# Prompt attention: gated heads first, stick and top-k heads in turn behind them, one output bank for each kind

## The chip, the cores and the metric

One core of a Trainium2 chip. The metric is the device time of one launch in microseconds, the median of the runs. TensorE multiplies and transposes, VectorE and ScalarE read its results from PSUM, GpSimd works on SBUF alone, and SP (SyncE) issues most of the DMA transfers. Each engine takes its instructions in the order in which the program lists them, and waits on semaphores.

## The reference

One step of a decoder layer for a prompt of 512 tokens and for 8 samples of 8 tokens over 4096 cached positions. Three groups of heads work on one projection of the normalised input: 4 stick-breaking heads, 6 heads with an index that selects 128 keys per query of the prompt, and 6 heads that add a compressed, a selected-block and a window branch with sigmoid gates. For the prompt it is, cut to what matters here:

```python
# stick-breaking, no softmax
z = q @ k.T * scale                                   # causal: k_pos < q_pos
log_keep = where(causal, log_sigmoid(-z), 0)
log_after = cumsum(log_keep, reverse=True) - log_keep
o_sb = where(causal, exp(log_sigmoid(z) + log_after), 0) @ v
# top-k ("dsa")
score = sum_heads(relu(iq @ ik.T) * iw)               # causal; top k keys of each query
o_dsa = softmax(q @ k_sel.T * scale + bias) @ v_sel
# gated ("nsa")
o_nsa = g0 * o_cmp + g1 * o_slc + g2 * o_win          # each a softmax with bias
out = concat(o_sb * silu(g_sb), o_dsa * silu(g_dsa), o_nsa * silu(g_nsa)) @ w_out
y = x + rmsnorm(out)
```

## The kernel before

The program does the projection, then the samples' attention, then `prompt_prepare`, `prompt_attention` and `finish` (the output projection with the norm). Each of these is a block of its own: all engines come together between two of them.

**`prompt_prepare`** turns 26 query and key tiles and 16 gate tiles of the projection, two at a time from 21 transfers (`PROMPT_LOADS`, a ring of 4 buffers), all issued by SP. ScalarE makes the sigmoids of the gates (Exp, Ln, Exp), VectorE multiplies them into `kept.oT` (L2291), and both copy the turned tiles. The index scores (`score`) are made between the tiles. The position bias of the twelve softmax heads comes in two transfers of six heads each (L2163): heads 6 to 11, the gated ones, ahead of load 10, and heads 0 to 5, the top-k ones, ahead of load 15. `mask` (L2277) adds the causal mask to the part of the bias that lies on the diagonal, on VectorE.

**`prompt_attention`** works through a list of 112 units. A unit is one head, one tile of 128 queries (`tile` 0 to 3, so 128 to 512 keys wide) and one branch:

- 16 stick units (4 heads);
- 72 gated units: for each of 6 heads and 4 tiles `slc`, `win`, `cmp`;
- 24 top-k units, `dsa` (6 heads), which need the finished top-k search.

Every engine runs one loop over the list. In iteration u:

- TensorE: score of u (L2438 to L2448) into one of 3 banks, turn of u-3 (L2463, L2460), product of u-5 with the values (L2477, L2474) into an `ov` bank;
- VectorE: `add(u)`, `invert(u-1)`, its copies of turned tiles of u-3 (L2497), the product with the gate when a head ends (L2634, six units behind), then its share of the top-k search (`best`, L2616 MAX8 and L2620 MATCH_REPLACE8: 96 steps in all, spread over the first 84 units);
- ScalarE: `exp(u)`, `exp_stick(u-2)`, its copies of u-3;
- GpSimd: `normalise(u-1)` for softmax units, and the padding of the window units.

A softmax unit goes: score, `add` on VectorE (logits plus bias with the maximum, L2589, signals `maxed`), one exp with its sum on ScalarE (L2542, waits for `maxed`), reciprocal on VectorE (L2606), normalisation on GpSimd (L2510, signals `ready`), turn. A stick unit goes: score, Abs, Exp, Ln on ScalarE (L2535 to L2537), three steps on VectorE (L2575 to L2579, signals `soft_dve`), one exp on ScalarE (L2546), turn. In code:

```python
def add(x):                                  # VectorE, a stick
    dve.wait_ge(soft_act, 3 * x.u + 3)       # ScalarE's Ln
...
def exp(x):                                  # ScalarE, a softmax unit
    act.wait_ge(maxed, x.u - n_stick + 1)
```

The output banks `ov[0]` and `ov[1]` alternate from head to head. The SP queue of this block copies the new rows of the caches to the outputs and loads the first three pieces of the output weights.

Of the kernel before, what the change touches and what calls it, by code (L numbers as in the profile page):

```python
# [20 lines left out]
ALU = mybir.AluOpType  # L21
ACT = mybir.ActivationFunctionType
AX = mybir.AxisListType

P = 128
D = 2048
SEQ = 512
# [2053 lines left out]
def prompt_prepare(nc, io, kept, keep):  # L2081
# [15 lines left out]
    with ExitStack() as ctx:  # L2097
# [14 lines left out]
        rows_in = kept.prompt_in  # L2112
        small_in, mask_in, bias_in = s.sem("small_in"), s.sem("mask_in"), [s.sem(f"bias_in{i}") for i in range(2)]
        biased, pad_step = s.sem("biased"), s.sem("pad_step")
# [140 lines left out]
        def _(dve):  # L2255
# [16 lines left out]

            def mask(first, at):

                dve.wait_ge(bias_in[0 if first else 1], 16)
                b = kept.bias[:, first:first + 6, at:at + P]
                dve.tensor_tensor(b, b, pm[:, at:at + P].unsqueeze(1).to_broadcast([P, 6, P]), ALU.add).then_inc(biased, 1)  # L2277

            def gate(i, n):
                if n == 13:  # L2280
                    mask(6, 0)
                    mask(6, SEQ)
                if n == 15:
                    mask(0, SEQ)
                if n == 16:
# [64 lines left out]
def prompt_attention(nc, io, kept, keep):  # L2350


    units = []
    for h in range(4):
        for i in range(4):
            units.append(Unit("stick", h, i, h, h, h, None, None, True, True))
    n_stick = len(units)
    for h in range(6):
# [19 lines left out]
    with ExitStack() as ctx:  # L2378
# [9 lines left out]
        cleared, scored, padded, maxed, exped, rcp_ready, ready = (  # L2388
            s.sem(n) for n in ("cleared", "scored", "padded", "maxed", "exped", "rcp_ready", "ready"))
        turned, copied, multiplied, out_done = s.sem("turned"), [s.sem("copied_dve"), s.sem("copied_act")], s.sem("multiplied"), s.sem("out_done")  # L2390
        soft_act, soft_dve, small = s.sem("soft_act"), s.sem("soft_dve"), s.sem("small")
# [5 lines left out]

        by_act = [u % 2 if u < n_stick else int(u % 3 > 0) for u in range(N)]

# [27 lines left out]
        def _(pe):  # L2427
            def score(x):
                if x.u >= SB:

                    before = units[x.u - SB]
                    if before.kind == "stick":
                        pe.wait_ge(soft_dve, 3 * before.u + 3)
                    else:
                        pe.wait_ge(maxed, before.u - n_stick + 1)
                q = kept.qT[:, x.q, x.tile * P:(x.tile + 1) * P]
# [14 lines left out]
            def turn(x):  # L2451
                if x.kind == "stick":
                    pe.wait_ge(exped, x.u + 1)
                else:
                    pe.wait_ge(ready, x.u - n_stick + 1)
                if x.u >= TB:
# [43 lines left out]
        def _(pool):  # L2500
# [3 lines left out]
            def normalise(x):  # L2504
                if x.kind == "stick":
                    return
                pool.wait_ge(rcp_ready, x.u - n_stick + 1)
                v = view(x)
# [3 lines left out]
            for u in range(N + 1):  # L2512
                if u < N and units[u].kind == "win":

                    pool.wait_ge(turned, u - LB + 1)
                    x = units[u]
# [6 lines left out]
        def _(act):  # L2523
# [3 lines left out]
            def exp(x):  # L2527
                if x.kind == "stick":

                    act.wait_ge(scored, x.u + 1)  # L2530
                    if x.u >= 2:

                        act.wait_ge(soft_dve, 3 * x.u - 3)
                    t = softs[x.u % 2][:, 0:x.w]
# [4 lines left out]
                act.wait_ge(maxed, x.u - n_stick + 1)  # L2539
                if x.kind == "win" and x.off:  # L2540
# [3 lines left out]
            def exp_stick(x):  # L2544
                act.wait_ge(soft_dve, 3 * x.u + 3)
                act.activation(view(x), view(x), ACT.Exp).then_inc(exped, 1)  # L2546

            for u in range(N + TURN):

                if u < n_stick:  # L2550
                    exp(units[u])
                if 2 <= u <= n_stick:
                    exp_stick(units[u - 2])
                if u == n_stick:
                    exp_stick(units[u - 1])
                if n_stick <= u < N:
                    exp(units[u])
                if u >= TURN and by_act[u - TURN]:
                    copy(act, units[u - TURN])

        @block.vector
        def _(dve):
            chain = Links(small)
            def add(x):
# [6 lines left out]
                if x.kind == "stick":  # L2571
                    t = softs[x.u % 2][:, 0:x.w]
                    z = sc[x.u % SB][:, 0:x.w]
                    dve.wait_ge(soft_act, 3 * x.u + 3)
                    dve.scalar_tensor_tensor(t, z, 0.0, t, ALU.max, ALU.add).then_inc(soft_dve, 1)  # L2575
                    dve.wait_ge(soft_dve, 3 * x.u + 1)
                    dve.tensor_tensor_scan(t[:, ::-1], t[:, ::-1], t[:, ::-1], 0.0, ALU.add, ALU.bypass).then_inc(soft_dve, 1)
                    dve.wait_ge(soft_dve, 3 * x.u + 2)
# [12 lines left out]
            def invert(x):  # L2591
                if x.kind == "stick":
                    return
                dve.wait_ge(exped, x.u + 1)
                r = rcp[:, x.u:x.u + 1]
# [26 lines left out]
            for u in range(N + MUL + 1):  # L2622
# [6 lines left out]
                if u - MUL - 1 in outs:  # L2629
# [3 lines left out]
                    to = kept.oT[:, x.out, :].rearrange("p (m t) -> p m t", m=4)  # L2633
                    dve.tensor_tensor(to, to, ov[place[x.out] % 2][:], ALU.mult).then_inc(out_done, 1)  # L2634
                if u < n_free:
                    for n in range(ops_until(u - 1), ops_until(u)):
                        best(n)
                if n_free - 4 <= u < n_free - 1:
                    i = u - (n_free - 4) + 1
# [389 lines left out]
```

## Time and profile before

| what | us |
|---|---|
| median of 3 runs (lowest, highest) | 2465.31 (2464.78, 2466.41) |
| the profiled execution, its own time | 2466.94 |
| its span, first to last instruction | 2465.1 |
| TensorE busy in it (mean granted clock 0.956) | 2276.2 |
| VectorE, ScalarE, GpSimd busy | 941.9, 856.5, 503.0 |
| attention of the prompt, from 2056.5 | 177.0 |

All times of rows are microseconds from the start of the span of one profiled execution. "PEclk" is the share of TensorE's full clock that was granted. In a group, "busy, mean ns of one | idle before it <- who ended that" follow each other; L numbers are lines of the kernel.

### The profile page before, as it was taken

How to read it: one execution, taken by the hardware profiler on the slowest of the kernel's cores; microseconds unless marked ns; L12 is line 12 of the kernel's file. 1: busy time of each engine (PE TensorE's matmuls, PEld its weight loads, DVE VectorE, ACT ScalarE, POOL GpSimd, SP SyncE). 2: the span in 40 equal slices, each digit the busy share in tenths (PEclk: the TensorE clock that was granted, in tenths of full speed). 3: DMA queues.
4: the chain of work that ended last, by engine and by line, in shares of the span. 5: the costliest groups of instructions: out<-in, count | busy, mean ns of one | idle time of the engine just before them, and what ended most of it. 6: DMA issues, size and time to landing. Idle time of an engine off the chain costs nothing. (4 is left out here: it accounts for less than half of the span.)

```text
span 2465.1 us, 46128 instructions
## 1 busy us (share of the span) xinstructions
PE 2276.2 (92%) x16622; PEld 1758.9 (71%) x16625; DVE 941.9 (38%) x1657; ACT 856.5 (35%) x1913; POOL 503.0 (20%) x403
## 2 busy tenths in 40 slices
PE   6999999999999999986999999788799867998996
PEld 3887777777777777764899999555555544777885
DVE  5111121212121212133588886533333348876123
ACT  4000332232222232211444443355455466662000
POOL 5433222222222222212200000000000000444332
PEclk7999999999999999998999999899899876999998
DMA  4755676767676767547666664899999876002423
GB/s 148 213 174 200 232 258 211 262 232 259 226 262 212 264 233 256 186 117 217 182 195 196 194 194 138 270 376 380 308 381 380 284 227 201 1 1 95 124 82 119
DMA packets 322723, 523.15 MB, mean 212 GB/s; under 512 B 36981, under 2 KB 128518, under 8 KB 320662
## 3 DMA queue, kind: packets, MB, share of 16 engines
q1 hardware_dynamic: 302722, 491.76, 60.0%
q10 hardware_dynamic: 16416, 23.13, 2.8%
q0 software_dynamic: 3360, 5.33, 0.6%
q8 instruction: 133, 2.18, 0.4%
q14 instruction: 92, 0.75, 0.1%
HBM read 497.83 MB, written 44.00 MB: 220 GB/s over the span
## 5 line engine op out<-in xcount | busy, mean ns | idle before, releaser
L549 POOL TENSOR_TENSOR proj_w_lo<-kept_region,proj_w_hi 128x1024 fp32r<-128x1024 f32 (+1 forms) x120 | 281.9, 2350 | 723.1 <-DVE proj_w_hi L796 723.1
L576 PE MATMUL proj_acc<-proj_w_hi,h_hi 128*128 128x512 f32 (+1 forms) x958 | 392.6, 410 | 0.0
L578 PE MATMUL proj_acc<-proj_w_lo,h_hi 128*128 128x512 f32 (+1 forms) x958 | 371.6, 388 | 0.0
L577 PE MATMUL proj_acc<-proj_w_hi,h_lo 128*128 128x512 f32 (+1 forms) x958 | 371.3, 388 | 0.0
L748 ACT COPY proj_kT<-proj_tp 128x512 f32<-128x512 f32 x256 | 150.4, 587 | 402.0 <-PE proj_tp L637 347.3
L796 DVE CAST proj_w_hi<-kept_region 128x1024 fp32r<-128x1024 f32 (+1 forms) x120 | 86.8, 726 | 385.5 <-PE proj_acc L580 382.8
L576 PEld LDWEIGHTS proj_acc<-proj_w_hi,h_hi 128*128 128x128 f32 x958 | 180.6, 189 | 60.9 <-issue 31.7
L578 PEld LDWEIGHTS proj_acc<-proj_w_lo,h_hi 128*128 128x128 f32 x958 | 180.2, 188 | 37.9
L577 PEld LDWEIGHTS proj_acc<-proj_w_hi,h_lo 128*128 128x128 f32 x958 | 181.1, 189 | 28.1
L1202 ACT COPY cmp_xT<-cmp_tp 128x512 f32<-128x512 f32 x260 | 139.0, 588 | 160.4 <-PE cmp_tp L1115 160.4
L637 PE MATMUL proj_tp<-kept_consts,kept_region 128*128 128x128 f32 x1024 | 153.5, 272 | 0.0
L637 PEld LDWEIGHTS proj_tp<-kept_consts,kept_region 128*128 128x128 f32 x1024 | 126.2, 140 | 35.5 <-ACT proj_kT L748 5.9
L1115 PE MATMUL cmp_tp<-kept_consts,kept_second 128*128 128x128 f32 x1040 | 139.3, 279 | 5.8 <-DMA kept_second<-in_cache_nsa_kv_dram 4.6
L974 DVE MAX8 kept_top<-kept_scores 64x8 f32<-64x4104 f32 x32 | 141.6, 4423 | 0.5
L976 DVE MATCH_REPLACE8 kept_scores<-kept_top,kept_scores 64x4104 f32<-64x4104 f32 x32 | 141.1, 4409 | 0.0
L1115 PEld LDWEIGHTS cmp_tp<-kept_consts,kept_second 128*128 128x128 f32 x1040 | 120.8, 144 | 8.0 <-DMA kept_second<-in_cache_nsa_kv_dram 5.7
L1173 PE MATMUL cmp_hp<-cmp_xT,kept_region 128*128 128x128 f32 x1024 | 125.9, 276 | 0.0
L1173 PE MATMUL cmp_hp<-cmp_xT,kept_w_values 128*128 128x128 f32 x1024 | 123.8, 275 | 0.0
L1173 PEld LDWEIGHTS cmp_hp<-cmp_xT,kept_region 128*128 128x128 f32 x1024 | 120.6, 193 | 0.0
L1173 PEld LDWEIGHTS cmp_hp<-cmp_xT,kept_w_values 128*128 128x128 f32 x1024 | 118.9, 192 | 0.0
L704 ACT COPY proj_out<-proj_acc 128x512 f32<-128x512 f32 (+1 forms) x60 | 34.6, 578 | 212.1 <-PE proj_acc L578 202.7
L2732 POOL TENSOR_TENSOR fin_w_lo<-kept_second,fin_w_hi 128x1024 fp32r<-128x1024 f32 x32 | 79.5, 2485 | 113.1 <-DVE fin_w_hi L2827 113.1
(458 smaller groups left out, 3637.3 us busy)
## 6 DMA issues: line engine op xcount, KB each, us to landing
kept_region<-in_cache_sb_kv_dram SPq DMA_DIRECT2D x256, 256.0 KB, 4.8
kept_second<-in_cache_sb_kv_dram SPq DMA_DIRECT2D x256, 256.0 KB
kept_second<-in_cache_nsa_kv_dram SPq DMA_DIRECT2D x512, 128.0 KB, 2.4
kept_region<-in_w_in_dram SPq DMA_DIRECT2D x112, 512.0 KB, 5.8
kept_region<-in_cache_nsa_kv_dram SPq DMA_DIRECT2D x128, 256.0 KB, 5.0
kept_region<-in_cache_dsa_kv_dram SPq DMA_DIRECT2D x128, 256.0 KB, 4.7
kept_second<-in_cache_nsa_kv_dram SPq DMA_DIRECT2D x64, 256.0 KB, 4.8
kept_rows<-in_cache_nsa_kv_dram SPq DMA_DIRECT2D x64, 256.0 KB, 5.2
```

What stands on the lines that cost most here:

```text
L549: pool.tensor_tensor(w_lo[p % SPLIT][:, :, here], w[p % RAW][:, :, here], w_hi[p % SPLIT][:, :, here], ALU.subtract).then_inc(lo_made, 1)
L576: pe.matmul(to, h_hi[:, kk, r], hi[:, k], start=first, stop=False)
L577: pe.matmul(to, h_lo[:, kk, r], hi[:, k], start=False, stop=False)
L578: last = pe.matmul(to, h_hi[:, kk, r], lo[:, k], start=False, stop=final)
L637: last = pe.transpose(tp[:, x:x + P], k_rows[:, b, p, h * DH:(h + 1) * DH], kept.ident)
L748: act.copy(kT[:, h % 2, 2 * pair:2 * pair + 2, :], tp[:].rearrange("p (b k) -> p b k", b=2)).then_inc(kT_copied, 1)
L796: dve.tensor_copy(w_hi[p % SPLIT][:, :, here], w[p % RAW][:, :, here]).then_inc(hi_made, 1)
L974: dve.max(kept.top8[:], kept.scores[:]).then_inc(kept.top_step, 1)
L976: dve.match_replace(kept.scores[:], kept.top8[:], kept.scores[:], GONE).then_inc(kept.top_step, 1)
L1115: last = pe.transpose(tp[n % 2 * 2 + a][:, p * P:(p + 1) * P], rows[i][:, p, a, :], kept.ident)
L1173: last = pe.matmul(hp[e][:, a, :], w1(2 * e + a, r), xT[:, 2 * e + a, r, :], start=(r == 0), stop=(r == CMPB - 1))
L1202: act.copy(xT[:, a, :, to], tp[n % 2 * 2 + own][:].rearrange("p (c r) -> p r c", r=CMPB)).then_inc(x_copied, 1)
```

## The change

The list of units begins with the 72 gated units. Behind them the 16 stick and 24 top-k units stand in groups of five: stick, top-k, stick, top-k, top-k. The top-k search is spread over the first 68 of the 72 gated units. Each unit gets a number within its kind (`nth`), by which the semaphores count, and the exp of a stick signals `stick_exped` instead of `exped`. Stick heads add up in bank 0 and top-k heads in bank 1; the gated heads alternate. A head waits for the head that held its bank before. The bias of the top-k heads is loaded at the start of the attention, first on SP's queue, and masked on VectorE half way through the gated units.

```diff
-                if i in (10, 15):
-                    first = 6 if i == 10 else 0
-                    src = bass.AP(io.lines.tensor, P - 1 + first * XL, [[HB * XL - 1, P], [XL, 6], [1, XW]])
-                    sp.dma_start(kept.bias[:, first:first + 6, :], src).then_inc(bias_in[i // 15], 16)
+                if i == 10:
+                    src = bass.AP(io.lines.tensor, P - 1 + 6 * XL, [[HB * XL - 1, P], [XL, 6], [1, XW]])
+                    sp.dma_start(kept.bias[:, 6:12, :], src).then_inc(bias_in, 16)
...
-                if n == 15:
-                    mask(0, SEQ)
...
-    for h in range(4):
-        for i in range(4):
-            units.append(Unit("stick", h, i, h, h, h, None, None, True, True))
-    n_stick = len(units)
     for h in range(6):
         for i in range(4):
             units.append(Unit("slc", 10 + h, i, 10 + h, 6 + h // 3, 6 + h // 3, 6 + h, 6 + h, True, False))
...
     n_free = len(units)
-    for h in range(6):
-        for i in range(4):
-            units.append(Unit("dsa", 4 + h, i, 4 + h, 4 + h // 3, 4 + h // 3, h, None, True, True))
+    sticks = [Unit("stick", h, i, h, h, h, None, None, True, True) for h in range(4) for i in range(4)]
+    chosen = [Unit("dsa", 4 + h, i, 4 + h, 4 + h // 3, 4 + h // 3, h, None, True, True) for h in range(6) for i in range(4)]
+    while sticks:
+        units += [sticks.pop(0), chosen.pop(0), sticks.pop(0), chosen.pop(0), chosen.pop(0)]
     N = len(units)
     for u, x in enumerate(units):
         x.u = u
+        x.nth = sum((y.kind == "stick") == (x.kind == "stick") for y in units[:u])
...
-    place = {units[u].out: n for n, u in enumerate(outs)}
+    bank, free_after, held = {}, {}, {}
+    for n, u in enumerate(outs):
+        x = units[u]
+        own = n % 2 if x.kind == "cmp" else int(x.kind == "dsa")
+        bank[x.out], free_after[x.out] = own, held.get(own, 0)
+        held[own] = n + 1
...
-        by_act = [u % 2 if u < n_stick else int(u % 3 > 0) for u in range(N)]
+        by_act = [x.nth % 2 if x.kind == "stick" else int(x.nth % 3 != 2) for x in units]
...
         def _(sp):
+            src = bass.AP(io.lines.tensor, P - 1, [[HB * XL - 1, P], [XL, 6], [1, XW]])
+            sp.dma_start(kept.bias[:, 0:6, :], src).then_inc(bias_in, 16)
             for to_p, to_s, col, width in io.new_rows:
...
-                if x.tile == 0 and x.first and place[x.out] >= 2:
-                    pe.wait_ge(out_done, place[x.out] - 1)
-                to = ov[place[x.out] % 2][:, x.tile, :]
+                if x.tile == 0 and x.first and free_after[x.out]:
+                    pe.wait_ge(out_done, free_after[x.out])
+                to = ov[bank[x.out]][:, x.tile, :]
...
             for u in range(N + TURN):
-                if u < n_stick:
+                if u < N:
                     exp(units[u])
-                if 2 <= u <= n_stick:
+                if 2 <= u < N + 2 and units[u - 2].kind == "stick":
                     exp_stick(units[u - 2])
-                if u == n_stick:
-                    exp_stick(units[u - 1])
-                if n_stick <= u < N:
-                    exp(units[u])
                 if u >= TURN and by_act[u - TURN]:
                     copy(act, units[u - TURN])
...
+                if x.kind == "dsa":
+                    dve.wait_ge(masked, 1)
...
+                if u == n_free // 2:
+                    dve.wait_ge(bias_in, 16)
+                    b = kept.bias[:, 0:6, SEQ:XW]
+                    dve.tensor_tensor(b, b, kept.pmask[:, SEQ:XW].unsqueeze(1).to_broadcast([P, 6, P]), ALU.add).then_inc(masked, 1)
```

## Rows read from the trace of the kernel before

**Rows 1.** Windows over attention; columns: us, busy by engine, clock, DMA.

```profile
2056.50:2099.60 43.10, 31.04 (x152) 20.88 (x152) 39.58 (x84) 31.01 (x71) 1.54 (x7) 0.82 0.66 205
2099.60:2191.20 91.60, 88.41 (x557) 67.28 (x556) 81.54 (x382) 58.54 (x188) 45.78 (x93) 1.00 0.01 1
2191.20:2233.50 42.30, 41.07 (x284) 34.19 (x285) 22.41 (x93) 22.43 (x71) 14.50 (x27) 1.00 0.00 1
```

**Rows 2.** Timeline of TensorE in the top-k stretch: two scores of tile 3.

```profile
2208.38 1.02 PE L2445 MATMUL pa_sc<-kept_kT,kept_qT 128*128 128x512 f32 x2
...
2214.35 1.02 PE L2445 MATMUL pa_sc<-kept_kT,kept_qT 128*128 128x512 f32 x2
```

**Rows 3.** Timeline: VectorE's first step of the attention.

```profile
2058.92 0.29 DVE L2575 SCALAR_TENSOR_TENSOR pa_soft<-pa_sc,pa_soft 128x128 f32<-128x128 f32 x1 [3.19 <-ACT pa_soft L2537]
```

**Rows 4.** Groups by line on VectorE, stick stretch (2056.5 to 2099.6).

```profile
L2577 DVE TENSOR_TENSOR_SCAN pa_soft<-pa_soft 128x128 f32<-128x128 f32 (+3 forms) x16 | 13.2, 824 | 0.5
L2579 DVE TENSOR_TENSOR pa_logits<-pa_sc,pa_soft 128x128 f32<-128x128 f32 (+3 forms) x16 | 7.9, 491 | 0.5
L2575 DVE SCALAR_TENSOR_TENSOR pa_soft<-pa_sc,pa_soft 128x128 f32<-128x128 f32 (+3 forms) x16 | 7.7, 479 | 3.2 <-ACT pa_soft L2537 3.2
```

**Rows 5.** Groups by line on ScalarE, same stretch.

```profile
L2536 ACT ACTIVATE pa_soft<-pa_soft 128x128 f32<-128x128 f32 (+3 forms) x16 | 7.5, 470 | 0.5
...
L2546 ACT ACTIVATE pa_logits<-pa_logits 128x128 f32<-128x128 f32 (+3 forms) x16 | 7.3, 455 | 2.8 <-DVE pa_logits L2579 2.8
L2535 ACT ACTIVATE pa_soft<-pa_sc 128x128 f32<-128x128 f32 (+3 forms) x16 | 6.9, 434 | 8.2 <-DVE pa_logits L2579 5.4 <-PE pa_sc L2448 2.7
```

**Rows 6.** Groups by line on ScalarE, top-k stretch (2192.5 to 2228.5).

```profile
L2542 ACT ACTIVATE pa_logits<-pa_logits,pa_nmax 128x128 f32<-128x128 f32 (+3 forms) x24 | 13.5, 561 | 16.1 <-DVE pa_nmax L2589 16.0
L2497 ACT COPY pa_pT<-pa_tp 128x512 f32<-128x512 f32 (+3 forms) x16 | 6.8, 425 | 0.0
```

**Rows 7.** Groups by line on VectorE, top-k stretch.

```profile
L2589 DVE CUSTOM_DVE_ANT_0 pa_logits<-pa_sc,kept_bias 128x256 f32<-128x256 f32 (+3 forms) x23 | 11.5, 500 | 15.4 <-PE pa_tp L2463 8.0 <-PE pa_sc L2445 6.1 <-PE pa_tp L2460 1.3
...
L2634 DVE TENSOR_TENSOR kept_region<-kept_region,pa_ov 128x512 f32<-128x512 f32 x5 | 3.4, 671 | 0.0
```

**Rows 8.** Timeline, top-k stretch: VectorE step, ScalarE step behind it.

```profile
2212.21 0.42 DVE L2589 CUSTOM_DVE_ANT_0 pa_logits<-pa_sc,kept_bias 128x256 f32<-128x256 f32 x1 [0.91 <-PE pa_sc L2445]
...
2212.67 0.51 ACT L2542 ACTIVATE pa_logits<-pa_logits,pa_nmax 128x256 f32<-128x256 f32 x1 [0.94 <-DVE pa_nmax L2589]
```

**Rows 9.** Groups by line on VectorE, gated stretch (2099.6 to 2191.2).

```profile
L2620 DVE MATCH_REPLACE8 kept_score<-pa_top,kept_score 128x512 f32<-128x512 f32 (+2 forms) x40 | 21.5, 539 | 0.0
L2616 DVE MAX8 pa_top<-kept_score 128x8 f32<-128x256 f32 (+2 forms) x39 | 20.7, 537 | 0.0
```

**Rows 10.** Timeline of the preparation, all engines.

```profile
2015.64 0.36 SPq L2163 DMA_DIRECT2D kept_bias<-bias_lines  x1
...
2024.78 1.94 PE L2220 MATMUL pp_gp<-kept_consts,kept_second 128*128 128x128 f32 x8 [3.10 <-DMA kept_second<-proj]
2025.90 0.60 ACT L2197 ACTIVATE pp_sig<-pp_gp 128x512 f32<-128x512 f32 x1 [2.02 <-PE pp_gp L2220]
...
2032.95 0.95 DVE L2277 TENSOR_TENSOR kept_bias<-kept_bias,kept_pmask 128x768 f32<-128x768 f32 x1
...
2034.15 0.69 DVE L2291 TENSOR_TENSOR kept_region<-pp_gp,pp_sig 128x512 f32<-128x512 f32 x1 [0.25 <-ACT pp_sig L2201]
```

**Rows 11.** Waits in the gated stretch; columns: total us, times, longest.

```profile
DVE pa_rcp L2606 <- ACT pa_logits L2542: 5.6, 18, 0.5
```

**Rows 12.** DMA issues, 1980 to 2060; last column: us to landing.

```profile
kept_bias<-bias_lines SPq DMA_DIRECT2D x2, 1920.0 KB, 9.0
```

**Rows 13.** Windows: the preparation's end, the attention's start.

```profile
2035.00:2054.00 19.00, 18.51 (x56) 10.64 (x56) 11.60 (x14) 8.04 (x14) 0.00 (x0) 0.50 0.51 167
2056.50:2062.00 5.50, 5.38 (x12) 2.63 (x13) 2.94 (x8) 5.02 (x11) 0.92 (x6) 0.50 0.75 241
```

**Rows 14.** The page: GB/s moved, in 40 slices of 61.6 us.

```profile
GB/s 148 213 174 200 232 258 211 262 232 259 226 262 212 264 233 256 186 117 217 182 195 196 194 194 138 270 376 380 308 381 380 284 227 201 1 1 95 124 82 119
```

More of the change, by code:

```diff
@@ L2112, in prompt_prepare @@
         rows_in = kept.prompt_in
-        small_in, mask_in, bias_in = s.sem("small_in"), s.sem("mask_in"), [s.sem(f"bias_in{i}") for i in range(2)]
+        small_in, mask_in, bias_in = s.sem("small_in"), s.sem("mask_in"), s.sem("bias_in")
         biased, pad_step = s.sem("biased"), s.sem("pad_step")
@@ L2271, in turn, with mask @@
                     dve.tensor_copy(kept.kT[:, n - n_q, :], tp[n % 4][:]).then_inc(copied_d, 1)
-            def mask(first, at):
-                dve.wait_ge(bias_in[0 if first else 1], 16)
-                b = kept.bias[:, first:first + 6, at:at + P]
+            def mask(at):
+                dve.wait_ge(bias_in, 16)
+                b = kept.bias[:, 6:12, at:at + P]
                 dve.tensor_tensor(b, b, pm[:, at:at + P].unsqueeze(1).to_broadcast([P, 6, P]), ALU.add).then_inc(biased, 1)
@@ L2280, in gate @@
                 if n == 13:
-                    mask(6, 0)
-                    mask(6, SEQ)
-                if n == 15:
-                    mask(0, SEQ)
+                    mask(0)
+                    mask(SEQ)
                 if n == 16:
@@ L2363, in prompt_attention @@
     n_free = len(units)
-    for h in range(6):
-        for i in range(4):
-            units.append(Unit("dsa", 4 + h, i, 4 + h, 4 + h // 3, 4 + h // 3, h, None, True, True))
+    sticks = [Unit("stick", h, i, h, h, h, None, None, True, True) for h in range(4) for i in range(4)]
+    chosen = [Unit("dsa", 4 + h, i, 4 + h, 4 + h // 3, 4 + h // 3, h, None, True, True) for h in range(6) for i in range(4)]
+    while sticks:
+        units += [sticks.pop(0), chosen.pop(0), sticks.pop(0), chosen.pop(0), chosen.pop(0)]
+    assert not chosen
     N = len(units)
@@ L2432, in score @@
                     if before.kind == "stick":
-                        pe.wait_ge(soft_dve, 3 * before.u + 3)
+                        pe.wait_ge(soft_dve, 3 * before.nth + 3)
                     else:
-                        pe.wait_ge(maxed, before.u - n_stick + 1)
+                        pe.wait_ge(maxed, before.nth + 1)
                 q = kept.qT[:, x.q, x.tile * P:(x.tile + 1) * P]
@@ L2452, in turn @@
                 if x.kind == "stick":
-                    pe.wait_ge(exped, x.u + 1)
+                    pe.wait_ge(stick_exped, x.nth + 1)
                 else:
-                    pe.wait_ge(ready, x.u - n_stick + 1)
+                    pe.wait_ge(ready, x.nth + 1)
                 if x.u >= TB:
@@ L2506, in normalise @@
                     return
-                pool.wait_ge(rcp_ready, x.u - n_stick + 1)
+                pool.wait_ge(rcp_ready, x.nth + 1)
                 v = view(x)
@@ L2513, in _ @@
                 if u < N and units[u].kind == "win":
-                    pool.wait_ge(turned, u - LB + 1)
+                    if u >= LB:
+                        pool.wait_ge(turned, u - LB + 1)
                     x = units[u]
@@ L2530, in exp @@
                     act.wait_ge(scored, x.u + 1)
-                    if x.u >= 2:
-                        act.wait_ge(soft_dve, 3 * x.u - 3)
-                    t = softs[x.u % 2][:, 0:x.w]
+                    if x.nth >= 2:
+                        act.wait_ge(soft_dve, 3 * x.nth - 3)
+                    t = softs[x.nth % 2][:, 0:x.w]
                     act.wait_ge(soft_act, chain.step(act.activation(t, sc[x.u % SB][:, 0:x.w], ACT.Abs)))
@@ L2538, in exp @@
                     return
-                act.wait_ge(maxed, x.u - n_stick + 1)
+                act.wait_ge(maxed, x.nth + 1)
                 if x.kind == "win" and x.off:
@@ L2544, in exp_stick @@
             def exp_stick(x):
-                act.wait_ge(soft_dve, 3 * x.u + 3)
-                act.activation(view(x), view(x), ACT.Exp).then_inc(exped, 1)
+                act.wait_ge(soft_dve, 3 * x.nth + 3)
+                act.activation(view(x), view(x), ACT.Exp).then_inc(stick_exped, 1)
             for u in range(N + TURN):
-                if u < n_stick:
+                if u < N:
                     exp(units[u])
-                if 2 <= u <= n_stick:
+                if 2 <= u < N + 2 and units[u - 2].kind == "stick":
                     exp_stick(units[u - 2])
-                if u == n_stick:
-                    exp_stick(units[u - 1])
-                if n_stick <= u < N:
-                    exp(units[u])
                 if u >= TURN and by_act[u - TURN]:
@@ L2571, in add @@
                 if x.kind == "stick":
[L2572 removed]
+                    t = softs[x.nth % 2][:, 0:x.w]
                     z = sc[x.u % SB][:, 0:x.w]
[L2574 removed]
+                    dve.wait_ge(soft_act, 3 * x.nth + 3)
                     dve.scalar_tensor_tensor(t, z, 0.0, t, ALU.max, ALU.add).then_inc(soft_dve, 1)
[L2576 removed]
+                    dve.wait_ge(soft_dve, 3 * x.nth + 1)
                     dve.tensor_tensor_scan(t[:, ::-1], t[:, ::-1], t[:, ::-1], 0.0, ALU.add, ALU.bypass).then_inc(soft_dve, 1)
[L2578 removed]
+                    dve.wait_ge(soft_dve, 3 * x.nth + 2)
                     dve.tensor_tensor(v, z, t, ALU.subtract).then_inc(soft_dve, 1)
@@ L2593, in invert @@
                     return
-                dve.wait_ge(exped, x.u + 1)
+                dve.wait_ge(exped, x.nth + 1)
                 r = rcp[:, x.u:x.u + 1]
@@ L2633, in _ @@
                     to = kept.oT[:, x.out, :].rearrange("p (m t) -> p m t", m=4)
-                    dve.tensor_tensor(to, to, ov[place[x.out] % 2][:], ALU.mult).then_inc(out_done, 1)
+                    dve.tensor_tensor(to, to, ov[bank[x.out]][:], ALU.mult).then_inc(out_done, 1)
                 if u < n_free:
```

2 lines of the change are left out of this document (added).

## The prediction

> **What bounds the kernel now.** I read the windows view over the attention first [rows 1], because the change reorders that stage and nothing that computes after it. The attention block runs from 2056.5 to about 2233.5 us, 177.0 us in three stretches. The reader is to see three different balances. In the stick stretch (43.1 us, 16 units) VectorE is busy 39.58 us: it is the bound, and TensorE has only 31.04 us of work at a mean clock of 0.82. In the gated stretch (91.6 us, 72 units) TensorE (88.41) leads and VectorE (81.54) is close behind. In the top-k stretch (42.3 us, 24 units) TensorE is busy 41.07 us and VectorE and ScalarE hardly half the time.
>
> The timeline of the top-k stretch gives TensorE's own pace: two scores of tile 3, four units apart, start 5.97 us from each other [rows 2], so 1.49 us a unit at the full clock. 24 units are 35.8 us; the other 6.5 us of the 42.3 are the edges (tail of the gated units, drain of the last head), and I keep them. Of the stick stretch 2.4 us are the fill, up to VectorE's first step at 2058.92 [rows 3]; 40.7 us are steady.
>
> A thing to notice before any busy share is added up: each engine takes its instructions in the order written. What two kinds of unit cost together is therefore not the larger busy sum unless no engine waits for another inside the loop.
>
> **The mixed stretch (40 units in eight groups stick, top-k, stick, top-k, top-k).** The prices are means over the four widths. VectorE, stick: 0.479 + 0.824 + 0.491 = 1.79 us [rows 4]. ScalarE before it: Abs 0.434, Exp 0.470, Ln the same 0.470 = 1.37 us; after it one exp, 0.455 [rows 5]. Top-k unit: ScalarE exp 0.561, a copy 0.425 on either engine [rows 6]; VectorE addition 0.500; the product with the gate at a head's end 0.671 [rows 7]. From a VectorE step to the ScalarE step that waits for it 0.04 us pass (2212.63 to 2212.67) [rows 8]; some ten such steps a group would be 0.4 us, which I leave to the range.
>
> Now the order in the changed code. ScalarE does in iteration u: exp(u), the stick exp of u-2, its copy of u-3. For a top-k unit exp(u) waits for `maxed`, that is for VectorE's add(u). VectorE reaches add(u) only after add(u-1), and when u-1 is a stick, that one waits for ScalarE's Ln and then takes 1.79. And the Abs, Exp, Ln of the next stick stand behind this exp(u) in ScalarE's queue. So ScalarE and VectorE take turns. In the stick stretch of before this did not occur: nothing that ScalarE does for stick u+1 waits for VectorE's work on stick u, which is why VectorE is 92% busy there [rows 1].
>
> One group, along the chain. First stick: 1.37 (ScalarE) + 1.79 (VectorE) + 0.50 (add of the top-k unit) + 0.56 (its exp) + 0.425 (ScalarE's copy of an earlier unit, before the next Abs) = 4.65. Second stick: 1.37 + 1.79 + 0.425 (VectorE's copy) + 0.50 + 0.425 (copy of the first stick) + 0.50 + 0.56 (exp of the last unit) + 0.455 (stick exp) + 0.425 (copy) = 6.45. Together 11.1 us. The ten products with the gate (0.67 each) fall on the chain in three iterations of five: 10 x 0.67 x 0.6 / 8 = 0.5. So 11.6 us a group and 8 x 11.6 = 93 us, against 40.7 + 35.8 = 76.5 us now: +16.5 us.
>
> Bounds of it. If no copy and no product with the gate lay on the chain, 11.1 - 4 x 0.425 = 9.4 us a group, 75 us, 1.5 us less than now. TensorE is off this chain at the full clock: five units are 7.5 of 11.6 us, and a score is issued up to three units ahead. It is the upper end that it sets: at half the clock five units are 14.9 us, 119 us in all.
>
> **The gated stretch, now first.** It takes the whole top-k search (96 steps, MAX8 and MATCH_REPLACE8) on VectorE in its 72 units, where 79 steps ran in it before [rows 9]. 17 steps at 0.54 are 9.2 us; the addition of the mask to the top-k heads' bias comes here too, 0.95 us [rows 10]. In sum +10 us: VectorE 81.5 + 10 = 91.5. Its waits for ScalarE before the reciprocal, 5.6 us in 18 places [rows 11], stay, since no search step stands between a compressed unit's addition and that reciprocal. So 97.1, and with half a microsecond of waits for TensorE 97.7, +6.1. Bounds: 91.6 if the waits are all filled (+0), 101.6 if all the 10 us of idle VectorE stay (+10).
>
> **The preparation.** The second bias transfer leaves the SP queue, 1920 KB, 9.0 us to landing [rows 12]. It was issued at 2015.64, right ahead of the next load, and TensorE sat 3.10 us before that load landed; ScalarE behind it sat 2.02 [rows 10]. ScalarE is the next engine in line, so I take 2.0, and 0.5 for matmuls that start sooner after other work: -2.5 us, between 0 and -5. Removing the mask's 0.95 us at 2032.95 saves nothing: VectorE's next product with a gate waited 0.25 us more for ScalarE [rows 10]. If that cover were gone it would save at most 0.95. What comes late then is TensorE's tail of turns and index scores, 18.51 busy of 19.0 us at clock 0.50, the 1.2 GHz level, after a stretch in which it had sat idle for loads and gates [rows 13]. It is only moved, not shortened; at the full clock it would be up to 9 us shorter, which I keep for the low end.
>
> **The start.** TensorE enters attention at 0.50 and stays there through 2062.0, 5.38 busy of 5.5 us [rows 13]. Now this falls on the gated units, where TensorE counts. Half of that work is 2.7 us; most of it hides behind the fill, 1 us is left: fill 3.4 instead of 2.4.
>
> **The moved bias transfer** is now first on SP in this block, ahead of ten copies to the outputs and the first loads of the output weights. Those wait about 5 us longer (1920 KB at the 380 GB/s that the page shows in its best slices), and nobody reads them before 2234; after about 2100 the queues are empty [rows 14]. I cost it at nothing. VectorE asks for the bias half way through the gated stretch, 36 units at 1.3 us = 47 us in, against 9 us to landing. Without that cover it would cost those 9.
>
> **The banks.** Before, two heads back had to be done; now a stick head waits for the stick head just before, and a top-k head for the top-k head before. The next head begins one to three units later and its product runs in the iteration behind the one with the gate's product, so TensorE waits for VectorE at some head ends. Below 0 it cannot be; at ten heads x 0.67 it is at most 6.7 us, and most of it falls in TensorE's free third. Taken as nothing.
>
> **The sum**, against the profiled execution (2466.94 us around a span of 2465.1): fill 3.4 + gated 97.7 + mixed 93 + edges 6.5 = 200.6 instead of 177.0, +23.6; with -2.5 from the preparation +21.1, 2488.0 us. The median of the runs is 1.6 us below that execution, so 2486.4, written 2486.
>
> **The rivals.**
> - *TensorE bounds the mixed stretch.* If the engines ran freely, it would need 40 x 1.49 = 59.7 us, against 53 on VectorE (39.6 - 9.2 + 22.4) and 53 on ScalarE [rows 1]: attention 3.4 + 97.7 + 59.7 + 6.5 = 167.3, with the preparation -12.2: 2453 us. For it: the busy sums. Against it: the order of the two queues. It decides from a group under 9.0 us, where the mixed stretch (71.9 us) pays for the gated one. The Trainium skill (Perfetto Trace Analysis, Optimization Strategy) says that where the most-contended engine changes over time, interleaving the regimes may improve the performance; the windows here do show such regimes, and the rule gives this rival's time.
> - *The chain is there but mostly covered.* Mixed 78, gated +2, preparation -5: attention 3.4 + 93.6 + 78 + 6.5 = 181.5, -0.5 in sum, about 2465; with half of each 2470 to 2476.
> - *TensorE's clock falls in the mixed stretch.* In the stick stretch it averaged 0.82 with TensorE busy 72% [rows 1]; in the new groups it is busy 65%. With half of the groups at 1.2 GHz, 4 x (14.9 - 11.6) = 13 us more: 2499; with all of them 2512.
>
> **How the numbers follow.** A measurement of this kernel tells 0.2%, 4.9 us, from no change (2460.4 to 2470.2). Chances: the chain as worked out 0.63 (own range 2476 to 2497), the clock 0.12, covered 0.12 (half of it within 0.2%), TensorE-bound 0.13. Faster 0.13, same 0.06, slower 0.81. The range 2466 to 2504 leaves out the TensorE-bound case and the far end of the clock's.
>
> **What the changed kernel's profile would show.** The mixed stretch some 90 us long, with VectorE near 55% busy, waiting at line 2575's counterpart for ScalarE's Ln, and ScalarE waiting at a top-k exp for `maxed`; neither waiting much for TensorE. The gated stretch 95 to 100 us with VectorE over 92%. The wait of 3.10 us for `kept_second<-proj` gone. The prediction is wrong if TensorE is over 90% busy at full clock in the mixed stretch, if VectorE's idle time there ends with TensorE, or if the preparation shortens by far more than 5 us.

## The result and the profile after

The changed kernel takes 2485.99 us (median of 6 runs, 2477.18 to 2491.32) against 2465.15 us of the kernel before in the same comparison: a ratio of 1.0084 (1.0071 to 1.0098), 20.8 us slower. The forecast was 2486.0.

The windows view of the changed kernel over its two stretches, with the columns of [rows 1]; the first stick's Abs starts at 2150.1:

```profile
2050.30:2150.10 99.80, 93.87 (x548) 69.73 (x549) 88.43 (x409) 60.66 (x192) 48.26 (x101) 0.95 0.34 109
2150.10:2252.40 102.30, 73.68 (x438) 55.59 (x442) 53.54 (x150) 51.24 (x139) 13.55 (x26) 0.95 0.00 1
```

The attention block takes 202.1 us (2050.3 to 2252.4) instead of 176.9. The gated stretch with the fill is 99.8 us (101.1 forecast); TensorE is busy 93.87 of it and VectorE 88.43, and TensorE's clock is 0.95 where [rows 1] show 1.00. The stretch of sticks and top-k units with its edges, called the mixed stretch, is 102.3 us (93 + 6.5 = 99.5 forecast). There VectorE is busy 52%, ScalarE 50% and TensorE 72%: no engine is the bound.

The waits in that stretch (waiting instruction, what ended the wait, us in total, times, longest):

```profile
ACT pa_logits L2548 <- DVE pa_nmax L2593: 42.0, 23, 3.3
DVE pa_soft L2577 <- ACT pa_soft L2543: 41.7, 16, 4.1
...
PE pa_ov L2482 <- DVE kept_region L2638: 12.3, 6, 2.7
...
ACT pa_soft L2541 <- PE pa_sc L2453: 1.8, 2, 1.0
```

VectorE sat 41.7 us in front of the 16 sticks until ScalarE's Ln, and ScalarE 42.0 us in front of exps of top-k units until VectorE's addition. Together these are 83.7 us of waiting of the one for the other in a stretch of 102.3. For TensorE's score ScalarE waited 1.8 us in all.

One group of five in the timeline (ScalarE and VectorE, the steps of the chain):

```profile
2173.64 0.28 ACT L2541 ACTIVATE pa_soft<-pa_sc 128x128 f32<-128x128 f32 x1
...
2174.29 0.31 ACT L2543 ACTIVATE pa_soft<-pa_soft 128x128 f32<-128x128 f32 x1
...
2174.70 0.29 DVE L2577 SCALAR_TENSOR_TENSOR pa_soft<-pa_sc,pa_soft 128x128 f32<-128x128 f32 x1 [2.51 <-ACT pa_soft L2543]
...
2175.49 0.29 DVE L2581 TENSOR_TENSOR pa_logits<-pa_sc,pa_soft 128x128 f32<-128x128 f32 x1
...
2175.76 0.54 DVE L2593 CUSTOM_DVE_ANT_0 pa_logits<-pa_sc,kept_bias 128x384 f32<-128x384 f32 x1
...
2176.34 0.62 ACT L2548 ACTIVATE pa_logits<-pa_logits,pa_nmax 128x384 f32<-128x384 f32 x1 [1.27 <-DVE pa_nmax L2593]
...
2177.10 0.38 ACT L2541 ACTIVATE pa_soft<-pa_sc 128x256 f32<-128x256 f32 x1
...
2177.97 0.42 ACT L2543 ACTIVATE pa_soft<-pa_soft 128x256 f32<-128x256 f32 x1
...
2178.49 0.42 DVE L2577 SCALAR_TENSOR_TENSOR pa_soft<-pa_sc,pa_soft 128x256 f32<-128x256 f32 x1 [2.18 <-ACT pa_soft L2543]
...
2180.08 0.40 DVE L2502 COPY pa_pT<-pa_tp 128x256 f32<-128x256 f32 x1
...
2180.40 0.68 DVE L2638 TENSOR_TENSOR kept_region<-kept_region,pa_ov 128x512 f32<-128x512 f32 x1
2181.00 0.68 DVE L2593 CUSTOM_DVE_ANT_0 pa_logits<-pa_sc,kept_bias 128x512 f32<-128x512 f32 x1
...
2181.72 0.72 ACT L2548 ACTIVATE pa_logits<-pa_logits,pa_nmax 128x512 f32<-128x512 f32 x1 [3.14 <-DVE pa_nmax L2593]
...
2183.79 0.49 ACT L2541 ACTIVATE pa_soft<-pa_sc 128x384 f32<-128x384 f32 x1
...
2231.83 0.49 ACT L2541 ACTIVATE pa_soft<-pa_sc 128x384 f32<-128x384 f32 x1
```

The reader is to see the hand-overs: Abs at 2173.64, Ln, VectorE at 2174.70 after 2.51 us of idleness, its addition of the next unit at 2175.76, that unit's exp at 2176.34 after 1.27 us of idleness, and only then the next Abs at 2177.10. The same again until 2183.79, and there a copy (2180.08) and a product with the gate (2180.40) stand on VectorE ahead of the addition, as the forecast's sum had them. This group holds the two narrowest sticks and takes 10.15 us. The last line is the first Abs of the eighth group. The tile view gives the first and the last of all 16:

```profile
L2541 ACT ACTIVATE pa_soft<-pa_sc x16: 260/436/597, 2150.1 to 2237.1; 128x128 f32<-128x128 f32 x4, 128x256 f32<-128x256 f32 x4, 128x384 f32<-128x384 f32 x4, 128x512 f32<-128x512 f32 x4
```

The first group starts at 2150.1 and the eighth at 2231.83: 81.7 / 7 = 11.7 us a group, where 11.6 were worked out. From the first stick to the last, which are seven groups and the first part of an eighth, are 87.0 us. Taking that first part at the forecast's 4.65 gives the same within 0.1: (87.0 - 4.65) / 7 = 11.8.

The preparation, from its first turned tile to the first clearing of the attention, before and after (tile views):

```profile
L2220 PE MATMUL pp_tp<-kept_consts,kept_second x116: 272/417/474, 1984.6 to 2053.1; 128*128 128x128 f32 x116
```

```profile
L2502 POOL MEMSET pa_logits<- x6: 194/196/205, 2056.6 to 2057.3; 128x128 f32 x6
```

```profile
L2219 PE MATMUL pp_tp<-kept_consts,kept_second x116: 272/421/478, 1980.2 to 2046.8; 128*128 128x128 f32 x116
```

```profile
L2507 POOL MEMSET pa_logits<- x6: 195/196/205, 2050.3 to 2051.0; 128x128 f32 x6
```

72.0 us become 70.1. The wait of 3.10 us for a load [rows 10] is not in the list of waits any more; one of 4.3 us for an earlier load is in both traces. The preparation also starts 4.4 us earlier in this trace, behind code that is the same in both; over the traces of this study it starts between 1979.0 and 1985.3. So the two profiled executions differ by +25.2 (attention), -1.9 (preparation), -4.4 (scatter ahead of it) and +0.3 behind it, 19.2 us of span.

### The profile page after: what moved, and what is told of

Same layout as the page of the kernel before. It is cut to its first block and busy times, and to the rows that moved or that the text cites. A ratio compares the mean times of both kernels' runs of the same rounds, so it can differ in the third digit from the quotient of the medians.

```text
span 2484.3 us, 46124 instructions
## 1 busy us (share of the span) xinstructions
PE 2281.5 (92%) x16619; PEld 1760.1 (71%) x16625; DVE 939.2 (38%) x1657; ACT 856.5 (34%) x1913; POOL 504.0 (20%) x403
```

## The experiments

All are edits of the changed kernel, but for the bias alone. They were timed in four sessions after that of the changed kernel, each with the kernel before beside them (medians 2463.5 to 2465.6), so the ratio compares two kernels more fairly than the medians do. The intervals are 0.1 to 0.25% to either side: the changed kernel, e4, e5, e9 and e10 (1.0065 to 1.0085) are not told from each other by time alone. The lengths in each profiled execution, from the first clearing to the first stick's Abs ("gated"), and from there to the end of the last product with the gate ("mixed"), with TensorE's granted clock:

| kernel | median us | ratio to before (95%) | gated (clock) | mixed (clock) |
|---|---|---|---|---|
| changed | 2485.99 | 1.0084 (1.0071 to 1.0098) | 99.8 (0.95) | 102.3 (0.95) |
| e1, Abs/Exp/Ln ahead | 2496.55 | 1.0135 (1.0120 to 1.0151) | 98.0 (0.95) | 112.2 (0.91) |
| e2, no turns | 2464.13 | 0.9995 (0.9986 to 1.0005) | 100.4 (0.92) | 77.9 (0.98) |
| e4, product first | 2481.60 | 1.0065 (1.0051 to 1.0080) | 98.1 (0.92) | 101.8 (0.90) |
| e5, two sticks together | 2483.71 | 1.0085 (1.0061 to 1.0109) | 103.4 (0.90) | 97.0 (0.93) |
| e8, both ahead | 2464.95 | 1.0003 (0.9992 to 1.0013) | 95.0 (0.96) | 83.5 (0.98) |
| e9, score ahead | 2482.81 | 1.0081 (1.0058 to 1.0104) | 95.1 (0.98) | 100.2 (0.88) |
| e10, 13 search rounds | 2481.88 | 1.0072 (1.0054 to 1.0090) | 93.7 (0.96) | 102.4 (0.95) |
| e11, both ahead, product first | 2464.43 | 1.0003 (0.9986 to 1.0021) | 92.5 (0.98) | 89.2 (0.90) |
| e12, both ahead, stick's exp early | 2454.04 | 0.9957 (0.9942 to 0.9972) | 94.9 (0.96) | 77.5 (0.98) |
| e13, two sticks, score ahead | 2468.49 | 1.0018 (1.0006 to 1.0030) | 95.3 (0.96) | 88.4 (0.92) |
| e14, stick's exp early alone | 2492.35 | 1.0115 (1.0098 to 1.0131) | 103.3 (0.90) | 105.4 (0.85) |

The lengths are of one execution each. In e11 (2471.19 us) and e12 (2459.41) that execution was 6.8 and 5.4 us longer than the median, in e1 (2492.88) and e10 (2478.74) 3.7 and 3.1 shorter; in the others it was within 3.

### Without the turns (e2)

```diff
-        units += [sticks.pop(0), chosen.pop(0), sticks.pop(0), chosen.pop(0), chosen.pop(0)]
+        units += sticks + chosen; sticks, chosen = [], []
...
-        own = n % 2 if x.kind == "cmp" else int(x.kind == "dsa")
+        own = n % 2
```

> The changed kernel, but behind the gated units all 16 sticks and then all 24 top-k units, and the banks alternating from head to head as before. Theory of the turns: sticks without the search take 8.8 us per four, 35 us in all, top-k units 36 us, so the two need 71 us instead of 93: attention about 178 us, time about 2464. Theory of the search: the gated stretch keeps nearly all of the loss, 2480 or more. If both count, the gated stretch is still 98 to 99 us, 6 to 7 more than before.

Measured 2464.13 us. The windows view of it, the same two stretches:

```profile
2049.60:2150.00 100.40, 94.61 (x548) 70.75 (x549) 88.74 (x409) 60.66 (x192) 48.28 (x101) 0.92 0.34 109
2150.00:2227.90 77.90, 67.14 (x441) 53.05 (x442) 55.20 (x150) 51.22 (x139) 13.56 (x26) 0.98 0.00 1
```

The gated stretch stays at 100.4 us and the rest falls from 102.3 to 77.9. The order of sticks and top-k units alone (with the banks that go with it) carries the whole loss. The denser search does not undo it: it is paid here too, in the gated stretch, and is made up for behind it. The sticks are rid of the search, and the stick and top-k stretches that took 43.1 + 42.3 = 85.4 us [rows 1] take 77.9 here.

### The bias alone (e3)

The kernel before, with the change's edits to `bias_in`, `mask` and `masked` and no other.

> The kernel before, with only the transfer of the top-k heads' bias and its mask moved into the attention. Expected from the preparation: 2 us less (0 to 5), from the mask on VectorE at most 1 more: 2463 to 2465. Rival, that the shift wakes TensorE's clock in the tail of the preparation: up to 9 us less, 2456.

Measured 2465.12 us, ratio 0.9997 (0.9987 to 1.0007). Its preparation, read as above:

```profile
L2219 PE MATMUL pp_tp<-kept_consts,kept_second x116: 272/418/475, 1984.8 to 2050.7; 128*128 128x128 f32 x116
```

```profile
L2502 POOL MEMSET pa_logits<- x6: 194/196/204, 2054.2 to 2054.9; 128x128 f32 x6
```

69.4 us instead of 72.0, -2.6. In the thirteen traces with the moved transfer (the changed kernel and the experiments) it is 68.2 to 70.7 us, the middle 69.6; without it there is one trace, the 72.0. The time of the whole kernel cannot tell 2.5 us (0.9990) from nothing; the traces can. TensorE's clock in the tail did not rise: it is 0.50 in every window of e3 from 2030 to 2054.

### Abs, Exp and Ln ahead (e1)

```diff
             for u in range(N + TURN):
-                if u < N:
+                if u + 1 < N and units[u + 1].kind == "stick" and units[u].kind != "stick":
+                    exp(units[u + 1])
+                if u < N and not (u and units[u].kind == "stick" and units[u - 1].kind != "stick"):
                     exp(units[u])
```

> The changed kernel, with ScalarE's Abs, Exp and Ln of a stick placed ahead of the exp of the softmax unit before it. Theory of the turns: the next stick's 1.37 us no longer stand behind an exp that waits for VectorE, so they run while VectorE works on the unit before. VectorE then needs about 6.9 us a group of five, ScalarE 6.6, TensorE 7.5; the mixed stretch falls from 94 us to between 60 and 75 and the time to 2452 to 2467. Theory of the banks (TensorE's 12.3 us of waits for the product with the gate set the stretch): it stays over 85 us, the time over 2476. Theory of the search (the denser search in the gated stretch is the loss): no change, 2486.

Measured 2496.55 us, 10.6 more than the changed kernel instead of 19 to 34 less. None of the three theories had this. Its waits in the mixed stretch:

```profile
DVE pa_soft L2579 <- ACT pa_soft L2543: 40.4, 16, 5.0
ACT pa_soft L2541 <- PE pa_sc L2453: 34.1, 15, 4.1
...
PE pa_tp L2468 <- ACT pa_logits L2552: 26.1, 13, 2.6
```

One place in its timeline:

```profile
2175.69 0.08 DVE L2595 DVE_READ_ACCUMULATOR2_ANT pa_nmax<- 128x1 f32 x1
...
2176.60 0.38 ACT L2541 ACTIVATE pa_soft<-pa_sc 128x256 f32<-128x256 f32 x1 [2.38 <-PE pa_sc L2453]
...
2177.79 0.60 ACT L2548 ACTIVATE pa_logits<-pa_logits,pa_nmax 128x384 f32<-128x384 f32 x1
```

ScalarE, which waited 1.8 us for stick scores, now waits 34.1 us in 15 places, and the exp of the unit at hand, already possible, waits behind. In the lines above its maximum is there at 2175.77, ScalarE sits 2.38 us for the next stick's score, and the exp comes at 2177.79. The score of u+1 is issued only after TensorE's turn of u-3 and product of u-5. So the early step met a score that was not there. My statement that TensorE is off the chain held for the chain as it stood, not for the one that this edit makes: the turns run through three engines.

### Both ahead (e8), the score ahead alone (e9)

To the edit above is added, in TensorE's loop:

```diff
-                if u < N:
-                    score(units[u])
+                if u == 0:
+                    score(units[0])
+                if u + 1 < N:
+                    score(units[u + 1])
```

> The changed kernel, with the Abs, Exp, Ln of a stick ahead of the exp before it, as in the first experiment, and TensorE's score of the next unit ahead of its turn and product. Theory of a ring of three engines (ScalarE, VectorE, and TensorE through the place of the score behind the turn): now the score lies ready, ScalarE's early work no longer blocks its queue, and the mixed stretch falls to 60 to 75 us, the time to 2452 to 2467. Rival, that the early Abs, Exp, Ln cost by themselves because they delay the exps that TensorE's turns need: the stretch stays over 90 us, 2480 or more.

> The changed kernel, with only TensorE's score of the next unit ahead of its turn and product. Theory of the turns between ScalarE and VectorE: TensorE is off the chain, at most 3 us less, 2482 to 2486. Rival, that TensorE's late scores are a good part of the mixed stretch: 8 us less or more, 2478 or below.

Measured 2464.95 and 2482.81 us. With both, the mixed stretch falls to 83.5 us, less far than the 60 to 75 expected, and the whole loss is gone: 18.8 us come from this stretch and 4.8 from the gated one. With the score alone the mixed stretch is 100.2 us, at a clock of 0.88. The waits of e8 in its mixed stretch:

```profile
DVE pa_soft L2581 <- ACT pa_soft L2545: 19.3, 13, 3.1
...
PEld pa_tp L2468 <- ACT pa_logits L2554: 12.2, 12, 1.7
...
ACT pa_soft L2543 <- PE pa_sc L2453: 5.9, 9, 0.8
```

VectorE's waits for Ln are 19.3 us instead of 41.7, and the new wait is 5.9 instead of 34.1. By its ratio (1.0081) e9 is not told from the changed kernel (1.0084). What its trace gains lies mostly in the gated stretch (95.1 instead of 99.8), where all four kernels with the score ahead and no other move on VectorE (e8, e9, e12, e13) stand at 94.9 to 95.3; the last section shows why.

### The product with the gate first (e4, e11)

The block with `out_done` on VectorE moves ahead of `add(units[u])`; in e11 on top of e8.

> The changed kernel, with VectorE's product with the gate at a head's end moved ahead of its addition for the current unit. Theory of the turns: only the ten products leave the chain, 4 us less, 2482. Theory of the banks: most of TensorE's 12.3 us of waits for that product go and the stretch shortens by 8 to 12 us, 2474 to 2478.

> Both moves ahead and the product with the gate ahead of VectorE's addition. If the chain is broken, the products matter as VectorE work alone and it is as fast as without this move, within 3 us; if the banks hold TensorE up, it is 5 us faster than without it.

Measured 2481.60, 4.4 us less than the changed kernel, and 2464.43, 0.5 less than e8. TensorE's wait for that product in e4:

```profile
PE pa_ov L2482 <- DVE kept_region L2632: 1.6, 2, 0.8
```

12.3 us have become 1.6, and the mixed stretch stands at 101.8 instead of 102.3. So the banks' waits were long, but most of them were not what the stretch waited for; the trace of e4, at a clock of 0.90 against 0.95, does not rule out a few microseconds. The 4.4 us agree in size with the products leaving the chain, but they are about the size of the uncertainty (ratios 1.0065 and 1.0084, intervals that overlap), and the profiled executions do not show them in that stretch; where they fell is not settled.

### Two sticks together (e5, e13)

```diff
-        units += [sticks.pop(0), chosen.pop(0), sticks.pop(0), chosen.pop(0), chosen.pop(0)]
+        units += [sticks.pop(0), sticks.pop(0), chosen.pop(0), chosen.pop(0), chosen.pop(0)]
```

> The changed kernel with the groups in the order stick, stick, top-k, top-k, top-k; nothing else. Theory of the turns: the second stick's Abs, Exp, Ln run while VectorE works on the first, and one exp of a top-k unit less stands between; a group is 9.3 us instead of 11.6, the mixed stretch 18 us shorter, 2468. Rival, that a stick anywhere among softmax units costs the same: no change, 2486.

> The groups stick, stick, top-k, top-k, top-k again, now with TensorE's score one unit ahead. Theory of a ring of three engines (the place of the score behind a turn that waits for the stick's exp closed the ring in the earlier run of this order): the 18 us that this order was to save appear now in good part, 2466 to 2472. Rival, that ScalarE's place of the stick's exp behind the exps of the top-k units holds the turns up by itself: 2478 to 2482.

Measured 2483.71 and 2468.49. e5 alone missed its 18 us (its ratio, 1.0085, is that of the changed kernel): 5.3 came in the mixed stretch, and its gated stretch, the same code, was 3.6 us longer at a clock of 0.90. Much of the miss in the mixed stretch has the cause of e1: with the score behind a turn that waits for ScalarE's stick exp, the next score comes late. With the score ahead the stretch is 88.4 us, 8.6 less, and the time 15 us below e5. The gated stretch, in which the score ahead helps by itself, is 8.1 us shorter too (95.3 instead of 103.4).

### The stick's exp early (e12, e14)

```diff
-                if 2 <= u < N + 2 and units[u - 2].kind == "stick":
-                    exp_stick(units[u - 2])
+                if 1 <= u <= N and units[u - 1].kind == "stick":
+                    exp_stick(units[u - 1])
```

This stands ahead of `exp(units[u])`; e12 has both steps ahead as well, e14 has not.

> Changed kernel, TensorE's score and ScalarE's Abs, Exp, Ln ahead as in the run that came down to the time of before, and the stick's exp one iteration earlier, ahead of the next exp. If the turns' waits for that exp (18 us on TensorE and its loads in that run) are on the path, the mixed stretch falls from 83 to 75 us or less and the time to 2455 to 2460. If TensorE's and VectorE's other work fills the time anyway, no change, 2465.

> The changed kernel with only the stick's exp one iteration earlier on ScalarE, ahead of the exp of the unit behind it; Abs, Exp, Ln and the scores stay in place. Theory of the turns: the exp stays on ScalarE's part of the chain, and the next stick's Abs, Exp, Ln still stand behind an exp that waits for VectorE; at most 5 us less, 2481 to 2486. Rival, that TensorE's wait for the stick's exp was the loss all along: 11 us less or more, 2475 or below.

e12 measured 2454.04 us, 0.9957 of the kernel before (0.9942 to 0.9972): the fastest version found, and faster than both kernels. The expectation was 75 us or less for the mixed stretch and 2455 to 2460 for the time. The windows view:

```profile
2053.40:2148.30 94.90, 90.22 (x547) 68.95 (x548) 87.61 (x408) 60.15 (x190) 47.94 (x100) 0.96 0.35 115
2148.30:2225.80 77.50, 67.78 (x446) 53.87 (x443) 53.51 (x150) 51.93 (x141) 13.87 (x26) 0.98 0.00 1
```

TensorE is busy 67.78 of 77.5 us, and no wait of it for a stick's exp is left in the list. In the traces the lead over e2, which does not mix the two kinds, lies in the gated stretch (94.9 instead of 100.4), where the score ahead acts, and not in the mixed one (77.5 and 77.9). The sequential order with the score ahead was not run; by the stretches of e9 and e2 it would take 95.1 + 77.9 = 173.0 us where e12 takes 172.4, an estimate from one trace each.

Alone (e14) the same move cost 6.4 us, which neither theory had. 3.5 of that stand in the gated stretch, whose code is untouched, at a clock of 0.90; 3.1 in the mixed stretch, at 0.85. ScalarE's waits moved from the top-k exps to the stick's exp. Whether the order or the lower clock made the 3.1 stays open.

### Three rounds of the search less (e10)

```diff
-        n_ops = TOPK_P // 8 * 6
+        n_ops = (TOPK_P // 8 - 3) * 6
```

> The changed kernel with 13 of the 16 rounds of the top-k search (78 steps instead of 96, so 24 keys less are selected for each query). Theory of the gated stretch bound by VectorE: 18 steps at 0.54 are 9.7 us of VectorE, and the stretch goes from 99 us back by 6 (2 to 10), time 2480. Rival, that TensorE sets the gated stretch and the search fits beside it: 1 us or less, 2485.

Measured 2481.88, 4.1 us less. The windows view of its gated stretch:

```profile
2049.00:2142.70 93.70, 90.73 (x548) 68.84 (x549) 81.29 (x382) 60.11 (x191) 48.52 (x101) 0.96 0.36 116
```

93.7 us instead of 99.8, 6.1 less, with VectorE at 81.29, where it stood in [rows 1]. The gated stretch of the same code took 98.0 to 103.4 us in five traces (last section), so one trace against another needs more than its length. VectorE's own account gives it; the waits of the changed kernel and of e10 in their gated stretches:

```profile
DVE pa_rcp L2610 <- ACT pa_logits L2548: 5.6, 14, 0.6
...
DVE pa_logits L2593 <- PE pa_sc L2450: 3.6, 4, 1.2
```

```profile
DVE pa_rcp L2610 <- ACT pa_logits L2548: 7.5, 20, 0.6
...
DVE pa_logits L2593 <- PE pa_sc L2450: 1.9, 5, 0.6
```

VectorE is busy 7.1 us less, waits 1.9 more for ScalarE ahead of the reciprocal, and 0.8 less for TensorE (scores and turns together): 6.0 of the 6.1. So the stretch follows VectorE's work. A step of the search comes out at 7.14 / 18 = 0.40 us of busy time, where the mean of its records is 0.54. Part of the difference is that each record overlaps the next by some 0.07 us in the timeline; the rest is not explained. In the time of the kernel the gain is 4.1 us by the medians and 3 by the ratios, within the uncertainty.

## Why the prediction was right

- **The reading of the windows** (three balances, no overlap gained by adding busy shares) held: VectorE and ScalarE end at 52% and 50%.
- **The chain.** 11.6 us a group forecast, 11.7 measured. Both long waits stand where they were said to: VectorE before the stick's first step for Ln, ScalarE before a top-k exp for `maxed`. e2 shows that the order costs 24 us in that stretch, and e8 that breaking the chain on two engines gives 19 of them back. The TensorE-bound rival (59.7 us for 40 units) never came: even e12 needs 77.5 with the edges. The Trainium skill (Perfetto Trace Analysis, Optimization Strategy) says that interleaving stretches with different most-contended engines may improve the performance. The changed kernel does not bear it out: 102.3 us interleaved, 77.9 one after the other. With e12's order of steps the interleaved stretch equals the sequential one (77.5 and 77.9), and no run here shows it gaining more.
- **A term too narrow in its reason.** "TensorE is off this chain" was right at the changed kernel (1.8 us of waits) but not a property of the loop: e1 made TensorE's score the late one. Once one link of a chain is moved ahead, the stretch is set by the link that comes next.
- **The gated stretch.** With the fill 99.8 instead of 101.1, but the terms behind it were off and cancelled. VectorE's busy time was put at 91.5 and is 88.43; by e10 a search step adds some 0.4 us and not 0.54. Its waits for TensorE were put at 0.5 and are 3.8. The waits before the reciprocal are 5.6, as forecast. The fill was put at 3.4 and is 0.9 up to VectorE's first addition (2051.24). So the sign "VectorE over 92%" did not come: it is 89%, and TensorE is at 94%. (The terms as written add up to 97.6, not 97.7.) e10 shortens the stretch by the forecast's 6.1 us, but as 7.1 of work less 1.1 of waits, where the forecast had 10 of work less 3.9 of waits.
- **The preparation.** -2.5 forecast, -1.9 in the trace after, -2.6 in e3, 69.6 as the middle of thirteen traces against 72.0. The time alone does not resolve it.
- **The banks**, taken as nothing with a bound of 6.7 us: the wait was 12.3 us, outside that bound as a wait. As a cost, e4 shows 4.4 us for it and the products together, with an uncertainty of about as much. The bound counted the product itself and not the additions ahead of it in VectorE's queue.
- **The clock.** In the mixed stretch it stayed at 0.95, so that rival did not come. It fell in the gated stretch instead, which the forecast had only at the start.
- **The moved transfer** cost nothing at the start of the attention: VectorE's masking ran at 2100.2 without a wait in the list:

```profile
L2645 DVE TENSOR_TENSOR kept_bias<-kept_bias,kept_pmask x1: 939/939/939, 2100.2 to 2100.2; 128x768 f32<-128x768 f32 x1
```

The edges and the mixed stretch came 2.8 us longer than forecast, the gated stretch 1.3 shorter. That the median falls on the forecast to 0.1 us is luck; the sum's own uncertainty is some 10 us.

## What to carry to other kernels

Before two kinds of unit are interleaved because their busy engines differ, walk one group through every engine's queue in order and add what hands over to what. Look for a step without a dependency (here Abs, Exp, Ln) that stands behind one with a dependency on the other engine. If such a step is moved ahead, its own input must be moved ahead with it, on the engine that makes it, or the queue blocks in the new place.

## What the runs showed that was not expected

TensorE's granted clock fell inside the gated stretch, in which it is nearly always at work. Windows of the changed kernel (columns as in [rows 1]):

```profile
2085.00:2090.00 5.00, 4.97 (x30) 3.53 (x28) 4.48 (x22) 2.12 (x8) 1.94 (x4) 1.00 0.03 12
2090.00:2095.00 5.00, 3.95 (x13) 2.62 (x14) 3.97 (x20) 2.65 (x9) 2.05 (x4) 0.68 0.00 0
2095.00:2100.00 5.00, 5.00 (x37) 4.09 (x35) 4.20 (x18) 3.44 (x11) 2.81 (x6) 0.98 0.00 2
```

It was busy 4.97 of 5 us at the full clock, then 3.95 of 5 at a mean of 0.68, so part of the time at the lower of its two levels, 1.2 GHz, and was back at 0.98. The gated stretch of the same code took 98.0 to 103.4 us (changed kernel, e1, e2, e5, e14) with mean clocks of 0.95 to 0.90; with the score ahead it took 94.9 to 95.3 at 0.96 to 0.98. VectorE's waits for the score show how the clock gets into the length. In the changed kernel all four lie in or just behind windows at a reduced clock (2090 to 2095 at 0.68; 2140 to 2145 at 0.80; 2145 to 2150 at 0.86):

```profile
2094.14 0.69 DVE L2593 CUSTOM_DVE_ANT_0 pa_logits<-pa_sc,kept_bias 128x512 f32<-128x512 f32 x1 [1.03 <-PE pa_sc L2450]
...
2145.66 0.69 DVE L2593 CUSTOM_DVE_ANT_0 pa_logits<-pa_sc,kept_bias 128x512 f32<-128x512 f32 x1 [1.17 <-PE pa_sc L2450]
...
2147.77 0.75 DVE L2593 CUSTOM_DVE_ANT_0 pa_logits<-pa_sc,kept_bias,kept_pad_least 128x512 f32<-128x512 f32 x1 [1.08 <-PE pa_sc L2450]
```

These waits and the lengths go together:

| kernel | VectorE's waits for the gated scores, us | gated stretch, us |
|---|---|---|
| e8, e9, e12, e13 (score ahead) | none | 94.9 to 95.3 |
| e1 | 1.7 | 98.0 |
| changed | 3.6 | 99.8 |
| e2 | 3.9 | 100.4 |
| e14, e5 | 6.5, 6.6 | 103.3, 103.4 |

e4, e10 and e11 change VectorE's work in this stretch and are left out.

With the score ahead a slow TensorE did not reach VectorE: e8 starts the attention at clocks of 0.50 and 0.70 in its first two windows of 5 us, and no wait of VectorE for a gated score is in its list. So the early score takes away most of what the low clock costs there. Why the clock falls in the middle of the stretch in the changed kernel, e2, e5 and e14, and not in e1 or in the kernel before (1.00 throughout its gated stretch), stays open.
